# Pooling mixer: the map of the raw stream, with the norm's reciprocals and the shift applied to its output; window masks made in the first FFN; the last inner tile by halves

## The chip, the cores and the metric

One core of one Trainium2 chip. The metric is device time in microseconds for one execution of the program. The engines are named as in the profile: PE is TensorE (matmuls), PEld its weight loads, DVE is VectorE, ACT is ScalarE, POOL is GpSimd, SP is SyncE, which here issues all DMAs.

## The reference, cut to what matters

A two-layer trunk over 1024 latent tokens (a 16 x 64 grid) of 1024 channels. Layer 0 has a recurrent mixer, layer 1 a pooling mixer; each layer then has a gated convolutional FFN with an inner width of 3072. In layer 1:

```python
h = modulate(rms_norm(x, norm_pre_mix), sh_m, sc_m)        # h * (1 + scale) + shift
for g, w in enumerate((2, 4, 8, 16)):                      # 256 channels each
    hg = h[..., g*256:(g+1)*256]
    pooled = window_sum_2d(hg, w) / (cr * cc)              # centred w x w window, clipped
    outs.append((pooled - hg) @ pool_w[g])
y = (concat(outs) + pool_b) * pool_scale
x = x + g_m * rms_norm(y, norm_post_mix)
x = x + g_f * rms_norm(conv_ffn(modulate(rms_norm(x, norm_pre_ffn), sh_f, sc_f)), norm_post_ffn)
```

and the FFN, in both layers:

```python
z = h @ w_up; u, v = z[..., :3072], z[..., 3072:]
u = depthwise_conv3(u) + bias
return (gelu(u) * v) @ w_down
```

## The kernel before, in words

Everything is held with channels on the 128 partitions: the stream X and the work tile Y are `[128, 8, 1024]`, eight channel tiles of 1024 tokens. A half h is 512 tokens (`hs(h)`). Norms are numbered q; q = 3 is the norm behind the first FFN, q = 4 the one ahead of the pooling mixer, q = 5 the one behind it, q = 6 the one ahead of the second FFN, q = 7 the last. `rb_bank` and `ssq_bank` give the PSUM banks of a norm.

**Order of the work.** Each engine has its own list of instructions, written out by hand, and the lists meet only at semaphores. Nothing is planned at run time, so an instruction that waits holds all that stands behind it on its engine. POOL can't read PSUM.

**A norm.** ACT squares the eight tiles (`square`, L1397). The squares are added up on DVE or POOL in one of several forms (`form`): `chain_sums` (L2305), `even_sum` (L2283) and `merge_sums` (L2289) on DVE, `odd_sum` (L1934) and `line_sums` (L1943) on POOL. `column_sums` (L831) on PE then sums over channels: per 512 tokens four fp32 matmuls with one moving column, 8 records in the trace. `norm_root` (L1401, ACT), `norm_scale` (L2320, the reciprocal, DVE) and `spread` (L878, PE), which puts the reciprocal of each token on all partitions of a PSUM bank, follow. Readers of that bank are `scale_tiles` (L2372) and `gate` (L2386) on DVE; `gate_tiles` also adds the even tiles to X (`add_even`, L2396), and POOL adds the odd ones (`add_odd`, L1972).

**FFN.** The loop body (`up`, L1171; `down_pair`, L1191) takes inner tiles in pairs, ten times. Weights and activations are split into high and low fp32r parts, three products each; the low parts of the weights are made on POOL and DVE. The 24th inner tile is alone (`last_up` on ACT and DVE, `down_last` on PE, `last_step` on POOL). Its convolution is a centre tap on ACT (`tap`, L1629), a left tap on DVE (`conv_left`, L2707), both 1024 wide, and a right tap by halves (`last_conv`, L2772). Then gelu (L1638), gate (L2779), high part (L1830) and low part (`last_lo`, L2783). PE's products go by 16 half tiles n (h, m = divmod(n, 8)), of which the first six are computed for the inner tile before and then, once `last_lo` is there, for the last one. DVE adds each to Y (L2631). During this stage `add_rows` (L1962) on POOL finishes the adaLN product of layer 1, out of rows `E_quad` that SP loads and ACT scales (`scale_rows`, L1776), and `later_coefs` on DVE makes its coefficients and the reciprocal window counts `cc` (L2617 to L2622).

**Norm 4.** For half 0 the eight squares are added on PE: `add_squares` (L871) multiplies them by the identity into bank 5, ACT copies the sum (L1870), column sums follow. For half 1 DVE adds six and PE's column sums take the last two.

**Pooling.** `z_tile(i)` (L1272) maps token tile i: out[token, channel] is the sum over k of Y[k, tokens]^T times pool_w, eight fp32 matmuls of 256 columns, into two banks; three pairs of banks are used in turn. Y is the normed, scaled and shifted stream: `scale_tiles(2, 4, h, X, False)` on DVE and `affine(h)` (L1858) on ACT. ACT rounds each result to ZT_hi (`z_hi`, L1864), DVE makes the remainder ZT_lo (`z_lo`, L2948). `window_sums(n)` (L1309, L1291) multiplies the transposed map by 0/1 band masks and count diagonals, 16 times; window 0 writes bank 0. POOL makes the masks (`edge`, L2215 to L2225; `band`, L2230, L2231, L2240) and the diagonals (L2251) behind the first FFN.

## Time and profile before

| | us |
|---|---|
| runs, unprofiled: median of 3 | 2013.16 |
| lowest, highest | 2013.06, 2017.11 |
| profiled execution | 2009.1 |
| its span (first to last recorded instruction) | 2007.4 |
| TensorE busy in it | 1953.0 (97%) |
| mean granted TensorE clock | 0.979 |

Times below are from the span's start. The first FFN's loop ends shortly before 1120, window sums run from 1217, the second FFN starts in the 1270s. A row of the timeline is start, duration, engine, line of the kernel, operation, output and inputs, count, and in brackets how long the engine was idle before it and which engine and instruction ended that. Rows of matmuls count two records per fp32 matmul.

### The profile page before, as it was taken

The page shows a single profiled execution, that of the slowest core. Times are in us where ns is not written, and L with a number is a line of the kernel's source. Part 1 is how long each engine was busy: PE and PEld are TensorE (multiplying, and loading weights), DVE is VectorE, ACT ScalarE, POOL GpSimd, SP SyncE. Part 2 cuts the span into 40 slices and gives each one's busy share as a digit, 9 for nine tenths or more (in the row PEclk, how much of TensorE's full clock was granted, in tenths as well). Part 3 has the DMA queues.
Part 4 walks back from the last instruction along what each step waited for, and adds up shares of the span by engine and source line. Part 5 has one row for each costly group of instructions (what it writes and reads, how often), then busy time and mean ns, then how long its engine had stood idle before and what let it go on. Part 6 is the DMA issues. An engine that isn't in the chain of part 4 may idle for free.

```text
span 2007.4 us, 27912 instructions
## 1 busy us (share of the span) xinstructions
PE 1953.0 (97%) x8766; PEld 1584.6 (79%) x8766; DVE 1669.3 (83%) x1781; ACT 997.8 (50%) x1425; POOL 1267.0 (63%) x846
## 2 busy tenths in 40 slices
PE   8999998999999999999999989899999999999997
PEld 3777776887888888888888768788888888888885
DVE  5588888978799989999998874897888888888888
ACT  5867668456444444444544455573343333343333
POOL 3544244665877778888877762465775655656765
PEclk9999999999999999999999989799999999999998
DMA  8322322540322232322222410211111111111114
GB/s 325 111 87 85 110 84 84 207 161 32 105 74 94 87 101 84 94 84 91 87 94 94 172 49 11 95 53 53 53 52 63 52 52 63 43 61 58 54 55 168
DMA packets 78016, 179.74 MB, mean 90 GB/s; under 512 B 5104, under 2 KB 28944, under 8 KB 77328
## 3 DMA queue, kind: packets, MB, share of 16 engines
q1 hardware_dynamic: 77968, 179.13, 26.1%
q8 instruction: 27, 0.44, 0.1%
q14 instruction: 21, 0.17, 0.0%
HBM read 166.52 MB, written 12.58 MB: 89 GB/s over the span
## 4 chain that ended last, share of the span: by engine, by line
PE 82%; ACT 7%; DVE 5%; issue 3%; POOL 2%; DMA 1%; SPq 1%; ACTq 0%; POOLq 0%; DVEq 0%
PE ps L1171 39%; PE ps L1191 19%; PE ps L772 14%; PE ps L997 2%; PE ps L1272 1%; PE ps L1309 1%; PE ps L831 1%; ACT TH L1524 1%; PE ps L1143 1%; DMA ada_first<-ada 1%; PE ps L878 1%; ACT RA L1527 1%; ACT TH L1534 1%; DVE Y L2386 1%; ACT L1534 1%
## 5 line engine op out<-in xcount | busy, mean ns | idle before, releaser
L2868 DVE TENSOR_TENSOR Y<-Y,ps 128x1024 f32<-128x1024 f32 x280 | 324.2, 1209 | 3.2
L2165 POOL TENSOR_TENSOR So_lo<-So_raw,So_hi 128x512 fp32r<-128x512 f32 x120 | 198.9, 1664 | 198.8 <-DVE So_raw L2804 167.7
L1730 ACT ACTIVATE So_hi<-So_raw 128x512 fp32r<-128x512 f32 x180 | 112.4, 625 | 148.4 <-POOL So_raw L2157 75.9
L1962 POOL TENSOR_TENSOR red<-red,E_quad 128x512 f32<-128x512 f32 x77 | 124.0, 1610 | 65.0 <-ACT E_quad L1776 62.2
L1915 POOL TENSOR_TENSOR WA_lo<-rawA,WA_hi 128x1024 fp32r<-128x1024 f32 x20 | 57.4, 2872 | 163.0 <-DVE u L2508 107.9
L1730 ACT ACTIVATE WB_hi<-rawB 128x512 fp32r<-128x512 f32 x120 | 74.6, 629 | 166.9 <-PE ps L1171 112.8
L1730 ACT ACTIVATE WA_hi<-rawA 128x512 fp32r<-128x512 f32 x120 | 73.1, 625 | 119.6 <-PE ps L1191 83.5
L1171 PE MATMUL ps<-T_hi,So_hi 128*128 128x512 f32 x336 | 131.3, 391 | 0.0
L1171 PE MATMUL ps<-T_hi,So_lo 128*128 128x512 f32 x336 | 130.8, 389 | 0.0
L1171 PE MATMUL ps<-T_lo,So_hi 128*128 128x512 f32 x336 | 130.7, 389 | 0.0
L1171 PE MATMUL ps<-H_hi,WA_hi 128*128 128x512 f32 x336 | 130.7, 389 | 0.0
L1171 PE MATMUL ps<-H_lo,WA_hi 128*128 128x512 f32 x336 | 130.7, 389 | 0.0
L1171 PE MATMUL ps<-H_hi,WA_lo 128*128 128x512 f32 x336 | 130.7, 389 | 0.0
L2165 POOL TENSOR_TENSOR WB_lo<-rawB,WB_hi 128x512 fp32r<-128x512 f32 x80 | 129.8, 1641 | 0.0
L2165 POOL TENSOR_TENSOR WA_lo<-rawA,WA_hi 128x512 fp32r<-128x512 f32 x80 | 104.4, 1305 | 3.8 <-ACT WA_hi L1730 3.8
L772 PE MATMUL ps<-H_hi,WA_hi 128*128 128x512 f32 x252 | 92.2, 412 | 9.0 <-DVE H_lo L2378 6.1
L1634 ACT ACTIVATE S<-S 128x1024 f32<-128x1024 f32 x46 | 48.8, 1062 | 94.6 <-DVE S L2713 94.6
L2856 DVE TENSOR_TENSOR Ub<-t,ps 128x512 f32<-128x512 f32 x84 | 57.8, 688 | 45.1 <-ACT t L1762 35.9
L2707 DVE SCALAR_TENSOR_TENSOR S<-Ub,par,S 128x1024 f32<-128x1024 f32 x48 | 84.4, 1759 | 9.3 <-ACT S L1629 9.3
L2856 DVE TENSOR_TENSOR t<-t,ps 128x512 f32<-128x512 f32 x84 | 57.3, 682 | 40.6 <-PE ps L1171 40.6
L772 PE MATMUL ps<-H_hi,WA_lo 128*128 128x512 f32 x252 | 88.3, 397 | 0.0
L772 PE MATMUL ps<-H_lo,WA_hi 128*128 128x512 f32 x252 | 88.2, 396 | 0.0
(437 smaller groups left out, 6317.8 us busy)
## 6 DMA issues: line engine op xcount, KB each, us to landing
rawA<-wA SPq DMA_DIRECT2D x62, 512.0 KB, 3.2
rawB<-wB SPq DMA_DIRECT2D x62, 512.0 KB, 3.3
E_quad<-ada SPq DMA_DIRECT2D x44, 512.0 KB, 3.4
quad<-ada SPq DMA_DIRECT2D x8, 2048.0 KB, 9.5
rawB<-wC SPq DMA_DIRECT2D x22, 512.0 KB, 3.8
rawA<-wC SPq DMA_DIRECT2D x20, 512.0 KB, 3.7
ada_first<-ada SPq DMA_DIRECT2D x8, 1024.0 KB, 15.1
outT<-X SPq DMA_DIRECT2D x16, 512.0 KB, 3.9
```

The source lines that it names most:

```text
L772: mm = pe.matmul(out, w[:, w_cols:w_cols + P], (hi, lo)[part], start=first and w is W_hi[s] and part == 0, stop=last and w is W_lo[s])
L997: mm = pe.matmul(out, gw[:, gi], src, start=True, stop=True)
L1171: mm = pe.matmul(ps[:, UP_OUT[name]], w[:, at + k * P:at + k * P + P], right[part][:, k], start=k == 0 and w is hi and part == 0, stop=k = ...
L1191: mm = pe.matmul(ps[:, DOWN_OUT[name][m]], w[:, at + m * P:at + m * P + P], TOKEN[name][part], start=name in ("11", "S1", "12") and w is h ...
L1634: A(S[0][:], S[0][:], ACT.Gelu_apprx_tanh).then_inc(gelu_done, 1)
L1730: A(dst[:, at:at + HF], op_source(name), ACT.Copy).then_inc(op_hi, 1)
L1915: TT(W_lo[s][:], raw[s][:], W_hi[s][:].bitcast(F32), ALU.subtract).then_inc(w_ready[s], 1)
L1962: TT(red[:], red[:], E_quad[:, :, k % 2 * P:k % 2 * P + P], ALU.add).then_inc(red_made, 1)
L2165: TT(lo[:, at:at + HF], op_source(name), hi[:, at:at + HF].bitcast(F32), ALU.subtract)\
L2707: STT(S[0][:], Ub[:, 0:T], col("ffn_conv_w", 72 * L + j), S[0][:], ALU.mult, ALU.add)\
L2856: TT(dst, a, b, op).then_inc(up_added, 1)
L2868: TT(at, at, ps[:, bank:bank + 2, :], ALU.add).then_inc(d_added, 1)
```

## The change

Four things.

1. The pooling map runs on X: A = (1 + scale) * norm weight is put into the weights (`pool_s`, made by ACT in `scale_map`), so z = rstd[token] * (X^T pool_s) + shift^T pool_w. `shift_map` on PE multiplies the shift, one column spread over 128 by broadcast, by pool_w into a bank per half, ACT copies it (`copy_shift`) to `z_shift`, and DVE applies reciprocal and shift in place in PSUM (`z_scale`). Tokens are on partitions there, so the reciprocal needs no spreading. `scale_tiles(2, 4, ...)`, `affine` and both `spread(4, ...)` go.
2. Norm 4's squares become lines on POOL with the rest in the column sums (five summed tiles of squares for half 0, three for half 1); `add_squares` goes. Norm 4's first sums stand behind z tile 0, the second behind z tile 3.
3. POOL makes the edges inside `last_step` of layer 0 and the bands between line sums; DVE makes the counts ahead of the last inner tile.
4. The last inner tile's taps go by halves in both layers (`last_tap`, `last_conv_left`, `last_conv`), PE's first products for it wait for u1 and not u3, and DVE's first two additions of its outputs stand before `last_lo(L, 1)`.

```diff
+        SCALED_BASE = {0: 0, 1: 16, 3: 32}
         def form(q, h):
-            if (q, h) == (4, 0):
-                return "acc"
             if q == 0:
                 return "pool"
-            if q == 1 or q and q % 2 == 0:
+            if q == 4:
+                return "line"
...
+        def line_end(q, h):
+            return 4 if (q, h) == (4, 0) else KT - 2
...
+            def shift_map(half):
+                bank = 5 - half
+                if half == 0:
+                    pe.wait_ge(poolw_full, 16)
+                    pe.wait_ge(coef_ready, 4)
+                pe.wait_ge(d_added, half_added("22", 0, PAIRS) + (16 if half else 13))
+                for g in (2 * half, 2 * half + 1):
+                    for k in range(2):
+                        c = (g % 2) * 512 + k * 256
+                        mm = pe.matmul(ps[:, bank, (g % 2) * 256:(g % 2) * 256 + 256],
+                                       M[:, 48 + 2 * g + k:49 + 2 * g + k].to_broadcast([P, P]),
+                                       pool_w[:, half, c:c + 256], start=k == 0, stop=k == 1)
+                mm.then_inc(z_done, 1)
...
 # down_last, PE
-                pe.wait_ge(up_added, added_at("u3", up))
+                pe.wait_ge(up_added, added_at("u1", up))
                 for n in range(6):
-                    if n > 3:
-                        pe.wait_ge(up_added, added_at(("v1", "v0")[n - 4], up))
+                    if n >= 3:
+                        pe.wait_ge(up_added, added_at(("u3", "v1", "v0")[n - 3], up))
...
+                if L == 0:
+                    shift_map(0)
                 square_sums(q, 1)
                 if L == 0:
-                    add_squares(4, 0, (0,))
+                    shift_map(1)
                 spread(q, 1)
...
-            add_squares(4, 0, range(1, KT))
-            norm(4, 0)
+            def z_tile(i):
                 b = 2 * (i % 3)
                 if i == 0:
-                    pe.wait_ge(poolw_full, 16)
+                    pe.wait_ge(zmap_made, KT)
+                if i == 2:
+                    pe.wait_ge(zmap_made, KT + 2)
                 if i >= 3:
                     pe.wait_ge(zt_lo, i - 2)
...
-                                       Y[:, 2 * g + k, i * P:i * P + P], pool_w[:, g // 2, c:c + 256],
+                                       X[:, 2 * g + k, i * P:i * P + P], pool_s[:, g // 2, c:c + 256],
...
-            for i in range(3):
+            z_tile(0)
+            square_sums(4, 0)
+            for i in range(1, 4):
                 z_tile(i)
             square_sums(4, 1)
-            z_tile(3, hook=True)
...
 # ACT
+            def last_tap(L, h):
+                j = FJ - 1
+                act.wait_ge(up_added, added_at("u1" if h else "u0", up_no(L, "A", PAIRS + 1)))
+                act.wait_ge(f_mul, DN * L + FJ - 1)
+                A(S[0][:, hs(h)], Ub[:, 1 + h * HF:1 + h * HF + HF], ACT.Identity, ...)
+            def scale_map(m):
+                act.wait_ge(poolw_full, 16)
+                act.wait_ge(coef_ready, 4)
+                c = m % 4 * 256
+                A(pool_s[:, m // 4, c:c + 256], pool_w[:, m // 4, c:c + 256], ACT.Copy, scale=cA[:, 2, m:m + 1])
...
+                    if L == 0 and 11 <= n < 15:
+                        scale_map(2 * n - 22)
+                        scale_map(2 * n - 21)
...
+            copy_shift(0)
             squares_x(4, 1, 0, (0,))
             norm_root(3, 1)
-            squares_x(4, 1, 0, range(1, KT))
...
+            squares_x(4, 1, 0, range(1, 4))
+            copy_shift(1)
+            squares_x(4, 1, 0, range(4, KT))
+            squares_x(4, 1, 1, range(4))
             norm_root(4, 0)
...
             squares_x(4, 1, 1, range(4, KT))
-            z_hi(1)
-            z_hi(2)
+            for i in range(3):
+                z_hi(i)
             norm_root(4, 1)
-            affine(1)
...
 # POOL
-                    for c in (2, 3):
-                        add_rows(PAIRS + 1, c)
+                    add_rows(PAIRS + 1, 2)
+                    window_edges()
+                    add_rows(PAIRS + 1, 3)
...
                 odd_sums(q, 0)
+                if L == 0:
+                    window_bands(range(3))
                 line_sums(q, 1, (1, 2, 3))
                 add_odd(i, 0, (1,))
                 line_sums(q, 1, (4, 5))
                 add_odd(i, 0, (3, 5, 7))
-                add_odd(i, 1, (1, 3, 5, 7))
+                if L:
+                    add_odd(i, 1, (1, 3, 5, 7))
...
+            line_sums(4, 0, (1, 2))
+            add_odd(1, 1, (1,))
+            line_sums(4, 0, (3,))
+            add_odd(1, 1, (3, 5))
+            line_sums(4, 1, (1,))
+            add_odd(1, 1, (7,))
+            line_sums(4, 1, range(2, line_end(4, 1)))
+            window_bands((3,))
...
+                if n in (2, 3, 4, 5):
+                    pool.wait_ge(z_done, KT + 2)
...
 # DVE
-                    gate_tiles(i, q, 1, range(4))
+                    gate_tiles(i, q, 1, range(KT))
                     norm_scale(4, 0)
...
                 pair_gated(L, "B", PAIRS)
+                if L == 0:
+                    window_counts()
+                last_conv_left(L, 0)
                 for name in ADDED[1:4]:
                     up_add(name, L, "A", p)
-                conv_left(L, FJ - 1)
-                up_add("u3", L, "A", p)
-                up_add("v1", L, "A", p)
                 last_conv(L, 0)
-                up_add("v0", L, "A", p)
+                last_conv_left(L, 1)
+                for name in ADDED[4:]:
+                    up_add(name, L, "A", p)
                 last_gated(L, 0)
+                last_lo(L, 0)
                 last_conv(L, 1)
-                last_lo(L, 0)
+                add_last(L, 0)
                 last_gated(L, 1)
+                add_last(L, 1)
                 last_lo(L, 1)
...
+            def z_scale(i, part=slice(0, D)):
+                dve.wait_ge(z_done, i + 3)
+                if i == 0:
+                    dve.wait_ge(zmap_made, KT + 2)
+                if i % 4 == 0:
+                    dve.wait_ge(rstd_made[i // 4], 5)
+                z = flat((AB01, AB23, AB45)[i % 3])[:, part]
+                STT(z, z, rstd[:, i:i + 1], z_shift[:, part], ALU.mult, ALU.add).then_inc(z_scaled, 1)
...
-            scale_tiles(2, 4, 0, X, False)
-            gate_tiles(1, 3, 1, range(4, KT))
-            chain_sums(4, 1, range(1, chain_end(4, 1)))
...
+            z_scale(0)
+            for i in range(1, 4):
+                z_scale(i)
+                z_lo(i - 1)
             norm_scale(4, 1)
+            z_lo(3)
+            z_scale(4)
+            for i in range(5, KT - 1):
+                z_scale(i)
+                z_lo(i - 1)
+            z_scale(KT - 1, hs(1))
+            z_lo(KT - 2)
+            z_scale(KT - 1, hs(0))
+            for half in (1, 0):
+                z_lo(KT - 1, hs(half))
```

## Rows read from the trace of the kernel before

**Rows 1.** The page's first part: busy time and share of the span by engine.
```profile
PE 1953.0 (97%) x8766; PEld 1584.6 (79%) x8766; DVE 1669.3 (83%) x1781; ACT 997.8 (50%) x1425; POOL 1267.0 (63%) x846
```

**Rows 2.** Windows: stretch, length, busy by engine, PEclk, DMA share, GB/s.
```profile
1179.40:1217.00 37.60, 36.49 (x161) 30.73 (x162) 25.08 (x32) 19.60 (x28) 20.00 (x34) 0.89 0.00 0
...
1164.00:1167.50 3.50, 3.50 (x12) 2.47 (x13) 3.50 (x5) 2.45 (x5) 1.64 (x2) 0.54 0.62 235
...
1177.40:1184.30 6.90, 4.92 (x12) 3.96 (x13) 6.90 (x12) 6.37 (x10) 0.41 (x1) 0.51 0.00 0
...
1194.50:1198.00 3.50, 3.50 (x12) 2.96 (x12) 0.39 (x2) 0.27 (x1) 3.50 (x5) 0.51 0.00 0
```

**Rows 3.** Timeline of PE, layer 0's end to the first window sum.
```profile
1137.65 0.47 PE L772 MATMUL ps<-WB_hi,WA_hi 128*128 128x512 f32 x1 [1.66 <-DVE WB_lo L2783]
...
1150.31 1.05 PE L831 MATMUL ps<-ones,V 128*128 128x1 f32 x8 [0.56 <-DVE V L2295]
...
1153.89 1.16 PE L878 MATMUL ps<-ident,rstd 128*128 128x128 f32 x8 [1.05 <-DVE rstd L2320]
...
1161.20 1.05 PE L831 MATMUL ps<-ones,V 128*128 128x1 f32 x8 [0.70 <-POOL V L1943]
...
1165.87 1.70 PE L878 MATMUL ps<-ident,rstd 128*128 128x128 f32 x8
...
1179.38 13.01 PE L1272 MATMUL ps<-pool_w,Y 128*128 128x256 f32 x48 [2.34 <-ACT Y L1858]
...
1205.57 11.49 PE L1272 MATMUL ps<-pool_w,Y 128*128 128x256 f32 x52 [0.18 <-ACT Y L1858]
1216.71 0.58 PE L1309 MATMUL ps<-band,ZT_hi 128*128 128x512 f32 x1
```

**Rows 4.** Timeline of ACT, 1140 to 1214.
```profile
1140.27 1.34 ACT L1776 ACTIVATE E_quad<-E_quad,silu_c 128x512 f32<-128x512 f32 x2
...
1210.19 1.02 ACT L1864 ACTIVATE ZT_hi<-ps 128x1024 fp32r<-128x1024 f32 x1 [2.43 <-PE ps L1272]
1213.64 1.02 ACT L1864 ACTIVATE ZT_hi<-ps 128x1024 fp32r<-128x1024 f32 x1 [2.43 <-PE ps L1272]
```

**Rows 5.** Timeline of DVE, 1128 to 1168.
```profile
1128.52 2.17 DVE L2707 SCALAR_TENSOR_TENSOR S<-Ub,par,S 128x1024 f32<-128x1024 f32 x1 [1.31 <-ACT S L1629]
...
1151.68 1.25 DVE L2619 TENSOR_SCALAR cc<-cc 128x32 f32<-128x32 f32 x1
...
1167.60 1.41 DVE L2386 SCALAR_TENSOR_TENSOR Y<-Y,cG,ps 128x512 f32<-128x512 f32 x2
```

**Rows 6.** Timeline of SP, and DMA issues 1100 to 1230 (size, time to landing).
```profile
1146.89 0.37 SPq L747 DMA_DIRECT2D pool_w<-poolw  x1
...
pool_w<-poolw SPq DMA_DIRECT2D x1, 1024.0 KB, 6.8
```

**Rows 7.** Timeline of POOL, and one group of 1140 to 1230 (busy, mean ns).
```profile
1141.07 2.73 POOL L1962 TENSOR_TENSOR red<-red,E_quad 128x512 f32<-128x512 f32 x2 [4.72 <-ACT E_quad L1776]
...
1165.47 1.58 POOL L1972 TENSOR_TENSOR X<-X,Y 128x512 f32<-128x512 f32 x1 [1.42 <-DVE Y L2386]
...
1187.95 0.53 POOL L2215 MEMSET edge<- 128x512 f32 x1
...
1192.98 0.30 POOL L2225 MEMSET edge<- 64x256 f32 x1
...
L1943 POOL TENSOR_TENSOR V<-V,S 128x512 f32<-128x512 f32 x4 | 5.2, 1290 | 1.9 <-ACT S L1397 1.6
```

**Rows 8.** Groups of DVE over the span: busy us, mean ns of one.
```profile
L2948 DVE TENSOR_TENSOR ZT_lo<-ps,ZT_hi 128x1024 fp32r<-128x1024 f32 x8 | 9.7, 1223 | 8.7 <-ACT ZT_hi L1864 8.6
...
L2386 DVE SCALAR_TENSOR_TENSOR ps<-Y,cG,ps 128x512 f32<-128x512 f32 x8 | 6.0, 756 | 1.1 <-PE ps L878 0.5
```

**Rows 9.** Timelines of DVE and PE, last inner tile of layer 1.
```profile
1961.40 2.99 DVE L2707 SCALAR_TENSOR_TENSOR S<-Ub,par,S 128x1024 f32<-128x1024 f32 x1 [1.32 <-ACT S L1629]
...
1965.13 0.47 PE L772 MATMUL ps<-F_hi,WC_hi 128*128 128x512 f32 x1 [0.34 <-DVE t L2856]
```

More of the change, by code:

```diff
@@ L104, in build_trunk @@
         sq0 = sb("sq0", [P, T])
-        W_lo = {"A": sb("WA_lo", [P, D], F32R), "B": sb("WB_lo", [P, D], F32R), "C": WC_lo}
+        W_lo = {"C": WC_lo}
+        W_lo["A"], = overlay(("WA_lo", [P, D], F32R))
+        z_shift = sb("z_shift", [P, D])
+        W_lo["B"] = sb("WB_lo", [P, D], F32R)
         S = [sb("S0", [P, T]), S1]
@@ L435, in form, with spreads_to @@
         def form(q, h):
-            if (q, h) == (4, 0):
-                return "acc"
             if q == 0:
                 return "pool"
-            if q == 1 or q and q % 2 == 0:
+            if q == 4:
+                return "line"
+            if q == 1 or q % 2 == 0:
                 return "chain"
             return "line" if q in (3, 7) and h else "tree"
+        def line_end(q, h):
+            return 4 if (q, h) == (4, 0) else KT - 2
+        def spreads_to(q):
+            return q - (q > 4)
         def adds_to(q, h, chain, pairs, tree=0):
-            each = {"chain": chain, "tree": pairs + tree, "line": KT - 3, "acc": 0, "pool": KT - 1}
-            return sum(each[form(n, h)] for n in range(q))
+            each = {"chain": chain, "tree": pairs + tree, "pool": KT - 1}
+            return sum(line_end(n, h) - 1 if form(n, h) == "line" else each[form(n, h)] for n in range(q))
         def chain_end(q, h):
@@ L458, in evens_to @@
         def evens_to(q, h):
-            each = {"tree": 3, "line": 0, "acc": 0, "pool": 0}
+            each = {"tree": 3, "line": 0, "pool": 0}
             return sum(chain_end(n, h) - 1 if form(n, h) == "chain" else each[form(n, h)] for n in range(q))
@@ L853, in square_sums @@
                     column_sums(q, h, *total, True, False)
-                    for p in (KT - 2, KT - 1):
+                    for p in range(line_end(q, h), KT):
                         pe.wait_ge(sq_made[h], 8 * q + p + 1)
@@ L1284, in window_sums @@
                     pe.wait_ge(band_ready, 3 * len(WINDOWS))
+                if n == 2:
+                    pe.wait_ge(zt_lo, KT + 1)
                 if n >= 4:
@@ L1385, in square @@
                         act.wait_ge(ssq_done[1], q)
-                    if (q, h) == (4, 0) and p > 3:
-                        act.wait_ge(acc_done, p - 3)
                 elif q == 0:
@@ L1767, in pair_tap @@
                 tap(L, 2 * p + 1 + "AB".index(s))
+            def scale_map(m):
+                act.wait_ge(poolw_full, 16)
+                act.wait_ge(coef_ready, 4)
+                c = m % 4 * 256
+                A(pool_s[:, m // 4, c:c + 256], pool_w[:, m // 4, c:c + 256], ACT.Copy, scale=cA[:, 2, m:m + 1])\
+                    .then_inc(zmap_made, 1)
             def scale_rows(q, c):
@@ L1818, in last_up @@
                 round_f(L, FJ - 2)
+                last_tap(L, 0)
                 round_down(L, FJ - 2)
```

145 lines of the change are left out of this document (67 added, 78 removed).

## The prediction

> **What bounds the kernel now.** The page's first part [rows 1]: TensorE is busy 97% of the span, so time comes off only where it idles, runs slowly, or does work that can go. The two FFN loops are full and hardly touched, so I read the stretches by stage [rows 2]. From 1160.5 to 1217.0, between the last down product of layer 0 and the first window sum, TensorE is poorly used: idle time in the first 18.9 us, and from the first z tile on a granted clock of 0.89. In the low stretches it is near 0.5, that is 1.2 GHz and not 2.4.
>
> TensorE's timeline [rows 3] gives the order. Products end at 1160.5 (0.70 idle before 1161.20). Then come norm 3's column sums, the adding of norm 4's squares by identity matmuls, norm 4's root, reciprocal and spreading, DVE's scaling, ACT's shift, and only then, at 1179.38, the first z tile. A z tile is 8 fp32 matmuls, 16 records, and costs 3.455 us at the full clock (ACT's ZT_hi, 1210.19 to 1213.64 [rows 4]). Eight are 27.6, but they last until 1217.06, since the second half waits for its own norm. Window sums start at 1216.71, and everything from there to the second FFN hangs on that start.
>
> **z stage.** The map now multiplies X itself. Removed are 16 scalings on DVE, 16 shifts on ACT, the identity matmuls and two spreads. How early can tile 0 start?
>
> - Before the products end, DVE loses the three count operations between its adds 9 and 10 (one took 1.25 at 1151.68 [rows 5]; about 1.6 with the other two and gaps). So norm 3's reciprocal is earlier, and the spread, which waited 1.05 [rows 3], waits no more: products end near 1159.3.
> - shift_map(0) is four fp32 matmuls 256 wide, half a z tile: 1.73, to 1161.0. It waits for pool_w, with the sums queued behind it; pool_w was issued at 1146.89 and landed after 6.8 [rows 6], 5 us ahead of need, and its place among SP's loads stays. Copying the result (128x512, 0.6) on ACT, with squares behind it, and the eight scale_map pieces (128x256 each) lie in idle gaps of the ACT.
> - Column sums of norm 3, right half: 24 records, which took 1161.20 to 1164.15. Again 2.95: 1164.0. The 1.2 us won before is spent.
> - shift_map(1): 1.73 at the full clock, 3.46 at half. Sums one column wide have let the clock fall: 0.54 granted from 1164.0, right after them [rows 2]. I take 3.4: 1167.4. Then the spread, 1.4 (1.70 when it lay partly in the low stretch [rows 3]): 1168.8. DVE began the gates that read it at 1167.60 [rows 5], so they lose 1.2.
>
> From here TensorE in order:
>
> - Tile 0: 3.46, to 1172.3. X of half 0 is complete; POOL's last addition to it ran from 1165.47 for 1.58 [rows 7].
> - Wait for POOL. Behind that addition stand two line sums, one X addition and a third line sum, each between 1.29 and 1.60 (the lower is the mean of a line sum [rows 7]): 1172.2 to 1173.5. DVE's own X additions contend, so I take 1173.3: a wait of 1.0.
> - Sums of norm 4, left half: one total and four squares, 40 records, 4.9 at full, 9.8 at half clock. The clock went down about 3 us after the earlier stretch of sums began [rows 2, 3]. Two fifths at full: 7.1, to 1180.4. The reciprocal follows at 1181; DVE has done the 12 gate and addition operations ahead of it by about 1178.
> - Tiles 1 to 3: 10.37, and 3 us at half clock at their start lose 1.6 (as from 1194.5 to 1198.0, at 0.51 [rows 2]): 1192.4.
> - Sums of norm 4, right half: 24 records, 2.95: 1195.3. POOL's five line sums for it are done by 1187.
> - Tiles 4 to 7: 13.82, and 1.5 lost in the same way: 1210.6.
> - The tail is new. Window sum 0 writes the banks of tile 6, and z_lo(6) stands on DVE behind the scaling of half of tile 7: 0.75 and 1.22 [rows 8], together 2.0: 1212.6. Before, the window sums followed with no gap.
>
> So the windows start at 1212.6 instead of 1216.7: **4.1 us earlier**.
>
> z_scale works in place in PSUM, 128x1024, a form that the trace lacks. It lies between 0.756, which a 512 wide one takes [rows 8], and twice that, 1.51; I take 1.3, nearer to twice. With z_lo's 1.22 DVE then needs 2.5 per tile against TensorE's 3.46. ACT needs 1.02. Tile and chain, 3.46 + 1.3 + 1.02 + 1.22 = 7.0, fit in the 10.4 that three buffers give. At either bound TensorE doesn't wait: nothing, beyond the tail.
>
> The masks' edges, ten operations from 1187.95 to 1193.28 [rows 7], were hidden under z tiles. They go to the 4.72 in which POOL waited for ACT ahead of E_quad's last addition [rows 7], and the bands to its waits for squares. No gain, and the last addition is 0.6 late; the matmuls that read its result come later. The diagonals in spare wait for the last z tile, with layer 1's first remainders behind them; those are needed only in the second FFN.
>
> **Last inner tile by halves, both layers.** In layer 0 TensorE waits 1.66 at 1137.65 for WB_lo [rows 3]. The chain behind it is tap, left tap (2.17 at 1128.52 [rows 5]), u3, v1, right tap. By halves a tap is 0.75 alone, so up to 1.7 could go. But POOL has WC_lo, WA_lo and two additions back to back there, and DVE operations with both operands in SBUF end just after one of POOL's: the left tap took 2.17 where twice 0.756 would do, and 2.99 in layer 1 [rows 9]. There are more such operations now, with the three counts ahead of u2. Walked through on that footing: counts to 1125.1, left tap 1128.1, u1 1130.0, right tap 1131.1, second left tap 1134.1, v0 1136.1, WB_lo 1138.8, which is 1.2 later than TensorE's start at 1137.65. Unblocked it is ready by 1135.8, 1.7 earlier. Either is met again: ACT's first square waits for E_quad until 1140.27 [rows 4], and the total of squares that TensorE wanted at 1150.31, idle 0.56 [rows 3], comes when it came. Price in layer 0: nothing, with bounds of 0.5 gained and 1 lost.
>
> The Trainium skill (SBUF — State Buffer, "SBUF: two separate sides") says that the port pair which DVE and GpSimd share is an exclusive lock: the second comer stands still for the first one's whole instruction. By that rule the walk to 1138.8 is the one that happens, and by free sharing the one to 1135.8. The trace leans to the lock, with 2.17 and 2.99 for the same operation.
>
> In layer 1 TensorE waited only 0.34, for u3 behind the 2.99 tap [rows 9]. It now needs u1 first, which was there before that tap began at 1961.40, and u3 only for its fourth product: **0.4 earlier**, and from there to the end TensorE and then DVE follow.
>
> **Sum.** 4.1 + 0.4 = 4.5. The profiled execution took 2009.1 (span 2007.4 and 1.7 around it), which gives 2004.6. The runs' median is 4.06 above it, so 2013.16 - 4.5 = **2008.7**. A measurement here can tell about 0.2%, 4.0 us, from no change; the forecast stands just beyond.
>
> **Rivals.**
>
> - *The clock holds better.* shift_map(1) takes 1.7 less, the spread 0.4 less, the left sums 2.2 less, tiles lose 1.5 less, and layer 0's halves give 0.5: up to 6 more than forecast. For it: the left sums have a full tile ahead of them. Against: after each stretch of sums in this stage the clock fell. Gain 6.5 to 11, middle 8.5: 2004.7.
> - *Absorbed.* All 40 records run at half clock (2.7 more), and the tiles after them stay at it for 7 us, as from 1177.4 to 1184.3 [rows 2] (1.9 more). That leaves 0 to 3, some 2012. For it: POOL is slowed by each of DVE's additions, and an idle TensorE brings the clock down sooner. If the change does not do what it says, because DVE's queue and not the norm held the first tile back, the time is here too.
> - *Slower, by the shared port.* In both layers DVE stands behind whole POOL operations in the last inner tile. Five of its operations (three taps, gate, remainder) by up to 2.4 make 12 per layer at most. It decides from 5.5 in sum, the gain of 4.5 and the 1 that layer 0 hides. At 4 per layer: 8 - 5.5 = 2.5 slower, 2015.7; up to 2018 with the counts in front. Against it: the u additions between them read PSUM and are not held.
>
> **Numbers.** Forecast case (gain 3 to 6.5, so 2006.6 to 2010.2) 0.45; better clock 0.22; absorbed 0.20; slower 0.13. The range over them is 2003.0 to 2014.0. Two thirds of the first case, 0.31, lie beyond 4.0: faster 0.22 + 0.31 = 0.53; same 0.14 + 0.20 = 0.34; slower 0.13.
>
> **What would show it.** Right: products end near 1159.3 and the first z tile starts near 1168.8; 40 records of sums take 5 to 9 us, in part at half clock; a gap of 2 before the first window sum, near 1212.6; WB_lo no earlier in layer 0; the loops the same. Wrong: sums at the full clock throughout; TensorE waiting over 2 us for POOL; a z tile waiting for z_lo; WB_lo over 3 late; products ending after 1160.5.

## The result, and the profile after

The changed kernel took 2018.04 us (median of 20 runs, 2013.49 to 2026.37), the kernel before 2012.17 on the same chip (20 runs). The ratio is 1.003, 95% interval 1.002 to 1.0039: **slower** by 0.3%, which is small but clear of the noise, where a gain of 0.2% was forecast. A second comparison (after_again, below) gave 1.004, 1.0028 to 1.0052. The profiled execution took 2018.32, its span is 2016.6; that of before was 2007.4, an execution 4 us under its median, so the 9.2 us between the two traces overstate the loss.

The page's first part [answers rows 1]:

```profile
PE 1956.5 (97%) x8782; PEld 1593.6 (79%) x8782; DVE 1677.2 (83%) x1772; ACT 991.4 (49%) x1421; POOL 1289.3 (64%) x854
```

TensorE's share says nothing. The windows by stage do: first before, then after (stretch, length, busy by engine, PEclk, DMA share, GB/s). The four stages are the products behind the second pass of the last tile, from there to the first z tile, the z tiles, and the window sums.

```profile
1137.60:1160.50 22.90, 21.23 (x102) 17.09 (x102) 19.98 (x37) 12.38 (x20) 12.60 (x10) 1.00 0.84 321
1160.50:1179.40 18.90, 14.60 (x66) 9.62 (x65) 13.52 (x21) 9.07 (x18) 8.31 (x6) 0.86 0.23 84
1179.40:1216.70 37.30, 36.19 (x160) 30.45 (x161) 25.08 (x32) 19.60 (x28) 20.00 (x34) 0.89 0.00 0
1216.70:1262.00 45.30, 43.16 (x287) 40.55 (x285) 24.77 (x37) 27.13 (x39) 16.41 (x11) 0.92 0.04 13
```

```profile
1139.50:1167.00 27.50, 23.98 (x103) 19.47 (x104) 21.09 (x35) 15.32 (x28) 19.68 (x23) 0.88 0.68 258
1167.00:1173.90 6.90, 6.90 (x50) 6.49 (x48) 5.92 (x10) 5.06 (x12) 4.16 (x4) 1.00 0.63 229
1173.90:1220.70 46.80, 41.58 (x195) 36.94 (x193) 29.67 (x31) 14.63 (x22) 26.14 (x28) 0.85 0.00 1
1220.70:1268.80 48.10, 45.96 (x284) 43.00 (x284) 25.40 (x39) 26.64 (x39) 16.34 (x11) 0.86 0.04 12
```

The products take 4.6 us longer, the way to the first z tile 12.0 less, the z tiles 9.5 more and the window sums 2.8 more, at 0.86 of the clock against 0.92. From the end of the products to the windows the trace of before has 56.2 us and this one 53.7: of the map's gain 2.5 are there. Ahead of it and behind it more than that goes.

TensorE's timeline [answers rows 3]:

```profile
1139.50 0.47 PE L783 MATMUL ps<-WB_hi,WA_hi 128*128 128x512 f32 x1 [1.81 <-DVE WB_lo L2847]
...
1154.23 1.05 PE L842 MATMUL ps<-ones,V 128*128 128x1 f32 x8 [2.63 <-DVE V L2347]
...
1166.88 1.89 PE L885 MATMUL ps<-pool_w,M 128*128 128x256 f32 x8
1168.60 0.95 PE L842 MATMUL ps<-ones,V 128*128 128x1 f32 x8
1169.41 1.93 PE L842 MATMUL ps<-ones,S 128*128 128x1 f32 x16
1171.20 1.97 PE L885 MATMUL ps<-pool_w,M 128*128 128x256 f32 x8
1173.01 1.05 PE L894 MATMUL ps<-ident,rstd 128*128 128x128 f32 x8
1173.90 3.62 PE L1288 MATMUL ps<-pool_s,X 128*128 128x256 f32 x16
1180.76 8.69 PE L842 MATMUL ps<-ones,sq 128*128 128x1 f32 x40 [3.25 <-POOL sq L1975]
1189.31 12.92 PE L1288 MATMUL ps<-pool_s,X 128*128 128x256 f32 x48
...
1204.66 14.06 PE L1288 MATMUL ps<-pool_s,X 128*128 128x256 f32 x64
1220.70 0.50 PE L1327 MATMUL ps<-band,ZT_hi 128*128 128x512 f32 x1 [1.97 <-DVE ZT_lo L3026]
```

TensorE's idle time has grown in three places: 2.63 for the total of norm 3's squares (0.56 before), 3.25 for GpSimd's line sum in the z stage, 1.97 ahead of the windows. Behind each of them stands a stretch at 1.2 GHz in which it is busy:

```profile
1157.20:1163.20 6.00, 5.36 (x17) 4.59 (x18) 3.25 (x7) 2.06 (x4) 3.83 (x3) 0.50 0.09 35
1177.50:1181.00 3.50, 0.25 (x3) 0.24 (x2) 3.50 (x5) 1.18 (x2) 3.50 (x4) 0.91 0.00 0
1181.00:1194.00 13.00, 13.00 (x51) 12.10 (x52) 5.86 (x6) 3.88 (x7) 11.50 (x10) 0.50 0.00 1
1221.70:1224.50 2.80, 2.80 (x8) 2.25 (x7) 0.89 (x2) 2.13 (x3) 1.54 (x1) 0.50 0.00 0
```

The long one, 13 us, holds all 40 sum records and the start of tile 1. Added up over the whole span in windows of 2 us, TensorE is busy at half clock for 59.5 us in the trace of before and for 74.5 in that of after: 15 more, and 7.5 of the 9.2 us are half of that. That the clock is lower holds beyond single traces: the granted clock, averaged over all executions, is 0.9785 for the kernel before and 0.9750 for the changed one.

Where the low stretches lie does not hold beyond single traces. The trace of after_again is a second one of the same changed kernel:

```profile
1169.99 3.48 PE L885 MATMUL ps<-pool_w,M 128*128 128x256 f32 x8
...
1179.06 7.98 PE L842 MATMUL ps<-ones,sq 128*128 128x1 f32 x40 [1.25 <-POOL sq L1975]
...
1217.56 0.50 PE L1327 MATMUL ps<-band,ZT_hi 128*128 128x512 f32 x1 [1.98 <-DVE ZT_lo L3026]
```

Here shift_map(1) runs at 1.2 GHz (3.48 in place of 1.97) and the wait for GpSimd is 1.25 in place of 3.25. The products behind the second pass take 25.3 us (27.5 in the first trace, 22.9 before), the way from their end to the windows 51.9, and the window sums 46.8, with no half clock behind the same gap of 2.0. The wait for the total is 2.65, as in the first trace. So a difference of one or two microseconds between stages of single traces can be chance, and the ratios decide.

Why the total is late shows in the queues of ScalarE and VectorE in the last tile [they answer rows 4 and 5]:

```profile
1141.87 0.63 ACT L1863 ACTIVATE WB_hi<-S 128x512 fp32r<-128x512 f32 x1 [1.16 <-DVE S L2843]
1142.52 1.28 ACT L1866 ACT_TABLE_LOAD   x1
1143.82 1.34 ACT L1808 ACTIVATE E_quad<-E_quad,silu_c 128x512 f32<-128x512 f32 x2
1145.06 0.61 ACT L1414 ACTIVATE V<-Y 128x512 f32<-128x512 f32 x1
```

```profile
1128.97 2.90 DVE L2836 SCALAR_TENSOR_TENSOR S<-Ub,par,S 128x512 f32<-128x512 f32 x1
1131.79 2.88 DVE L2830 SCALAR_TENSOR_TENSOR S<-Ub,par,S 128x512 f32<-128x512 f32 x1
...
1138.56 0.80 DVE L2847 TENSOR_TENSOR WB_lo<-S,WB_hi 128x512 fp32r<-128x512 f32 x1 [0.76 <-ACT WB_hi L1863]
1139.28 0.77 DVE L2836 SCALAR_TENSOR_TENSOR S<-Ub,par,S 128x512 f32<-128x512 f32 x1
1140.47 0.69 DVE L2684 TENSOR_TENSOR Y<-Y,ps 128x512 f32<-128x512 f32 x1 [0.42 <-PE ps L783]
1141.08 0.76 DVE L2843 TENSOR_TENSOR S<-S,V 128x512 f32<-128x512 f32 x1
```

ScalarE runs from its second WB_hi through the table load and E_quad to the first square without a pause: the square comes 3.19 behind the start of WB_hi. And WB_hi waits for the gate of the second half. On VectorE the right tap that this gate needs now stands behind WB_lo of the first half, which itself waits for ScalarE (before, the tap came first), and between tap and gate stands an addition that waited 0.42 for TensorE. In the kernel before, the same queue (E_quad's row is in [rows 4]):

```profile
1138.98 1.28 ACT L1833 ACT_TABLE_LOAD   x1
...
1141.52 0.62 ACT L1397 ACTIVATE V<-Y 128x512 f32<-128x512 f32 x1
```

There the table load began 1.33 after the second pass, now 3.02 after it.

### The profile page after: what moved, and what is told of

It reads as the page before. It is cut to its first block and busy times, and to the rows that moved or that the text cites. A ratio compares the mean times of both kernels' runs of the same rounds, so it can differ in the third digit from the quotient of the medians.

```text
span 2016.6 us, 27965 instructions
## 1 busy us (share of the span) xinstructions
PE 1956.5 (97%) x8782; PEld 1593.6 (79%) x8782; DVE 1677.2 (83%) x1772; ACT 991.4 (49%) x1421; POOL 1289.3 (64%) x854
## 5 line engine op out<-in xcount | busy, mean ns | idle before, releaser
L2223 POOL TENSOR_TENSOR So_lo<-So_raw,So_hi 128x512 fp32r<-128x512 f32 x120 | 208.0, 1740 | 200.1 <-DVE So_raw L2868 169.0
L783 PE MATMUL ps<-H_hi,WB_hi 128*128 128x512 f32 x220 | 79.3, 402 | 5.8 <-ACT Y L1554 3.9
```

What stands on the lines that cost most here:

```text
L783: mm = pe.matmul(out, w[:, w_cols:w_cols + P], (hi, lo)[part], start=first and w is W_hi[s] and part == 0, stop=last and w is W_lo[s])
L2223: TT(lo[:, at:at + HF], op_source(name), hi[:, at:at + HF].bitcast(F32), ALU.subtract)\
```

## The experiments

All ratios are against the kernel before on the same chip, with 95% intervals; "clock" is the granted clock averaged over all executions of a kernel.

**e1_whole: the halves undone.** VectorE's end of queue is that of the kernel before again, with one centre tap and one left tap, and TensorE's first products wait for u3 again; map, masks and counts stay. VectorE's part:

```
-last_conv_left(L, 0)
 for name in ADDED[1:4]:
     up_add(name, L, "A", p)
+conv_left(L, FJ - 1)
+up_add("u3", L, "A", p)
+up_add("v1", L, "A", p)
 last_conv(L, 0)
-last_conv_left(L, 1)
-for name in ADDED[4:]:
-    up_add(name, L, "A", p)
+up_add("v0", L, "A", p)
 last_gated(L, 0)
+last_conv(L, 1)
 last_lo(L, 0)
-last_conv(L, 1)
-add_last(L, 0)
 last_gated(L, 1)
-add_last(L, 1)
 last_lo(L, 1)
```

> The changed kernel with one part undone: the last inner tile is convolved whole again (one centre tap, one left tap), and VectorE's queue ends as in the kernel before. Map, masks, counts stay. Theory A (the last tile's new order on VectorE lets ScalarE's second WB_hi, its table load and so the squares of norms 3 and 7 come late, and the products wait for the total of the squares and then run at half clock): products of the last tile, from WB's pass to their end, fall from 27.5 to about 23 us in layer 0 and from 21.4 to about 20 in layer 1; the time comes to about 1.000 of the kernel before, 2012. Theory B (the window counts on VectorE, or the lock between VectorE and GpSimd, delay it): the stage stays near 27 us and the time at 1.003, 2018. Theory C (the window edges on GpSimd delay its sums): as B.

Ratio 1.0011 (1.0 to 1.0023), clock 0.9757: some 0.2% of the loss goes. Layer 1's products are back at 19.9 us from 21.4. Layer 0's are 26.5, not 23: the wait for the total fell from 2.63 only to 1.56, and a stretch at half clock still followed. So the halves in this order cost, and something else in the same stage does too.

**e2_before_halves: the kernel before with the halves alone** (the same edit the other way round).

> The kernel before with this one part added: the last inner tile's taps by halves and the new order on VectorE in both layers. Theory A: the products after the second pass of the last tile take 4 to 5 us longer in layer 0 and about 1.5 in layer 1, and the time is 1.002 to 1.003 of the kernel before. Theories B and C: nothing of it is in this kernel, so the ratio is 1.000.

Ratio 0.9998 (0.9986 to 1.0009), clock 0.9785. Theory A's time is refuted here, and its mechanism is not: the trace shows the wait for the total at 2.54 and products of 26.8 us. But the second pass began 1.8 us earlier relative to the tile's first product (4.1 against 5.9 us), and the way to the first z tile was 2.1 shorter (16.8 against 18.9), since VectorE and ScalarE set that stage and not TensorE. So in this kernel the loss is covered by other queues. That it lies bare once the map has taken their work away is read from the two traces.

**e3_order: the halves kept, VectorE's order as before.**

```
 last_gated(L, 0)
-last_lo(L, 0)
 last_conv(L, 1)
-add_last(L, 0)
+last_lo(L, 0)
 last_gated(L, 1)
-add_last(L, 1)
 last_lo(L, 1)
+add_last(L, 0)
+add_last(L, 1)
```

> The changed kernel with the taps still by halves, but the end of VectorE's queue in the order of the kernel before: gated 0, last_conv(1), WB_lo(0), gated 1, WB_lo(1), and both additions behind them. Theory A, in its narrow form (it is the order, not the split taps): second WB_hi on ScalarE about 1.2 us earlier, the wait of the products for the total at most 1 us, the stage 23 to 24.5 us, time 1.000 to 1.001. If the split taps themselves are what costs, the stage stays at 26 or more and the time at 1.002 to 1.003.

Ratio 1.0008 (0.9996 to 1.0019), clock 0.9765. Products 23.45 in layer 0 and 19.72 in layer 1, wait for the total 1.11 and no half clock in the stage: the narrow form of theory A holds. It was the order and not the split. The way from the products' end to the windows was 55.6 us in this trace, which is of an execution 3 us above its kernel's median.

**e6_sums: norm 4's left sums behind the second z tile.**

```
 z_tile(0)
+z_tile(1)
 square_sums(4, 0)
-for i in range(1, 4):
+for i in range(2, 4):
     z_tile(i)
```

> The changed kernel with TensorE's sums of norm 4, first half, behind the second z tile in place of the first. Theory D (TensorE waits 3.3 us there for GpSimd's last line sum while there is work for it): the wait goes, the z stage from its first product to the windows is 2 to 3 us shorter, the time 1.001 to 1.002 of the kernel before. Rival: VectorE's scaling of the first tile needs the same norm and becomes the wait, so that the stage is less than 1 us shorter and the time stays at 1.003.

Ratio 1.0015 (1.0002 to 1.0029), clock 0.9759. The wait for GpSimd is gone, the z tiles take 40.2 us from the first to the windows in place of 46.8 (43.4 in the changed kernel's second trace), and no z tile waits for VectorE. The rival (VectorE becomes the wait) falls.

**e10_map: the map alone**, with the tile whole, the counts behind the coefficients, and edges and bands behind the line sums on GpSimd.

```
 line_sums(4, 1, range(2, line_end(4, 1)))
-window_bands((3,))
+window_edges()
+window_bands(range(4))
```

> The kernel before with the mixer's map and its sums alone: last tile whole, window counts behind the coefficients, window masks behind the line sums on GpSimd, as in the kernel before or behind its new work. Theory F (what is lost is TensorE's clock: its mean over all executions fell from 0.9785 in the kernel before to 0.975 in the changed one, the same as before with the halves alone, so the fall comes with the map's stage, where TensorE now stands 3.3 us for GpSimd's line sum and runs the 40 columns behind it at half clock): the stage from the end of the products to the windows is 2 to 3 us shorter than before's 56.2, the mean clock 0.976, the time 1.000 to 1.001. Rival (my prediction's sum for the map was right, and the masks, counts and halves ahead of it lose it): 0.998 of the kernel before, clock 0.978 or more.

Ratio 0.9998 (0.9988 to 1.0008), clock 0.9772. Products 22.9, as before; the wait for GpSimd is 3.25 and the gap ahead of the windows 1.97 here as well. The map as written gains nothing, and it holds neither the whole loss nor the forecast gain. Theory F's time came true and its stage did not: from the products' end to the windows the trace has 57.1 us and not 2 to 3 less than 56.2. That trace is of an execution 6 us above the kernel's median, and its last four z tiles hold 6.5 us at half clock.

**e5_masks: only edges and bands moved back** in the changed kernel, as above.

> The changed kernel with the window masks behind the line sums on GpSimd in place of inside the first feed-forward part. Theory C (4.8 us of edges ahead of the odd sums and 4.3 us of bands behind them make GpSimd late for X's additions and its line sums of norm 4): TensorE's wait for GpSimd in the z stage falls from 3.3 us to 1 or less, time 1.001 to 1.002. Theory F with the masks hidden: wait and ratio as in the changed kernel, 1.003, or more if the masks now end after the z tiles.

Ratio 1.0017 (1.0008 to 1.0026), clock 0.9758. By the ratios the masks cost 0.13 to 0.23%, with overlapping intervals against the changed kernel's first ratio and none against its second. Theory C's time holds. Its wait for GpSimd was 1.07, but that does not bear it out: shift_map(1) ran at half clock here (3.34), and the changed kernel itself has 1.25 where it does so. The wait for the total was still 2.19. Their mark is on VectorE, ahead of the reciprocal that the spread waits for; VectorE and then GpSimd in the changed kernel:

```profile
1154.88 0.75 DVE L2407 SCALAR_TENSOR_TENSOR cA<-M,par 128x8 f32<-128x8 f32 x2
1155.56 1.26 DVE L2413 TENSOR_TENSOR dM<-M 128x4 f32<-128x4 f32 x1
```

```profile
1154.40 1.13 POOL L2190 TENSOR_TENSOR band<-edge 128x448 fp32r<-128x448 f32 x1
1155.52 1.28 POOL L1975 TENSOR_TENSOR V<-V,acc 128x512 f32<-128x512 f32 x1
```

cA starts beside a band and ends with it; dM, of 4 columns, runs exactly as long as GpSimd's addition, which the bands have made to follow without a pause. Here, with the bands gone, dM takes 0.15.

**e4_counts: only the three counts moved back.**

```
-if L == 0:
-    window_counts()
 last_conv_left(L, 0)
```

> The changed kernel with the window counts on VectorE behind the coefficients again. They are three small instructions of 0.2 us; theory B (they hold up the left tap, and what hangs on it) allows 0.6 us twice at most: time 1.0025 to 1.003. All other theories: 1.003, as the changed kernel.

Ratio 1.0027 (1.0015 to 1.0039), clock 0.9754: no effect that could be told. The counts are not 0.2 us each where the change puts them: in the changed kernel they take 1.27, 1.23 and 0.19. The second pass did begin 2.5 us earlier (4.1 against 6.6 us behind the tile's first product), and the products, still waiting for the total, took 26.2.

**e9_best: three mends in the changed kernel.** The order of e3, the sums of e6, and in VectorE's queue:

```
-z_scale(KT - 1, hs(1))
 z_lo(KT - 2)
+z_scale(KT - 1, hs(1))
 z_scale(KT - 1, hs(0))
```

> The changed kernel with three mends: end of VectorE's queue in the order of the kernel before (as e3_order), sums of norm 4 behind the second z tile (as e6_sums), and on VectorE the remainder of tile 6 ahead of the scaling of tile 7. Theory F: products of the last tile in 23.5 us, end of products to windows in 48 to 49 us (before 56.2), so 6 to 7 us less than the kernel before in these stages; if the clock stays at 0.976 to 0.977 half of that is given back and the ratio is 0.998 to 0.999. Rival (any saving there is given back in full by the clock of the windows and of the second feed-forward part): 1.000 or more, with a mean clock of 0.975.

Ratio 0.996 (0.9945 to 0.9974), clock 0.9788: more than the better of the two forecasts. Products to windows 47.15 (56.2 before), window sums 45.2. The clock is back at that of before (0.9784 on this chip).

**e12_no_tail: without the third mend.**

> Of the three mends only two: VectorE's order and the sums behind the second z tile; the remainder of tile 6 stays behind the scaling of tile 7. The gap ahead of the windows was 2.0 us in both e6_sums and the changed kernel. If the mend of the tail is worth its shorter gap (about 0.5 us) the ratio is 0.996; if it is what let the clock stay up in the windows, 0.998 or more.

Ratio 0.998 (0.9969 to 0.9992), clock 0.9779. TensorE's first window sum, in e12_no_tail and then in e9_best:

```profile
1218.28 0.50 PE L1327 MATMUL ps<-band,ZT_hi 128*128 128x512 f32 x1 [1.97 <-DVE ZT_lo L3027]
```

```profile
1215.27 0.50 PE L1327 MATMUL ps<-band,ZT_hi 128*128 128x512 f32 x1 [0.25 <-DVE ZT_lo L3027]
```

The gap goes from 1.97 to 0.25. Exchanging two operations was worth 4 us by the ratios, though their intervals leave anything from nothing to 9; 1.7 are the gap. The window sums (46.7 against 45.2 us) differ by 1.5 more, but not right behind the gap: there both run at full clock, and the longer low stretch is some 23 us later (1241.5 to 1252 against 1240 to 1247). Over all traces the window sums take 46.6 to 48.2 us behind a gap of 2 (ten traces, mean 47.4) and 45.2 to 46.9 without it (seven, mean 46.1); five of the ten have 3 to 3.5 us at half clock right behind the gap, five have none. So the gap seems to cost about a microsecond beyond its length, on average and not each time.

**e13_best_whole: e9_best with the tile whole.**

> The mended kernel (e9_best) with the last tile convolved whole, VectorE's queue as in the kernel before; masks and counts stay early. With the masks early and the tile whole the products took 26.5 us in e1_whole, against 23.5 with the halves in e3_order. If that difference belongs to the halves (they bring the additions no earlier, but the squares of the second half less late), the stage is again 25 us or more and the ratio 0.997 to 0.998. If it was the chance of one clock fall, 23.5 to 24 us and 0.996, as e9_best.

Ratio 0.997 (0.996 to 0.998), products 26.5 again. Here the halves are worth 0.1% in the right order. With the masks behind the sums and the counts behind the coefficients it is the other way: e16_best_counts, with halves, has 0.9963, and e15_map_mended, without them and otherwise the same, 0.9955. The intervals overlap in both pairs, so no worth of the halves is shown.

**e11_best_masks: e9_best with the masks moved back.**

> The mended kernel (e9_best) with the window masks behind the line sums again. Theory C (the masks on GpSimd hold VectorE's small operations and the sums: even sum 0.87 in place of 0.69 us, dM 1.27 in place of 0.15): products 23 us or less, wait for the total under 0.5 us, time 0.995 of the kernel before. Rival: behind the line sums the masks end after the z tiles or slow VectorE's work there, and the ratio is 0.997 or more.

Ratio **0.9945** (0.9932 to 0.9959), 2000.28 us median of 6, clock 0.9802: the fastest kernel of all, 11 us under the kernel before. Its windows by stage, as above:

```profile
1137.60:1159.00 21.40, 20.97 (x103) 17.50 (x104) 18.40 (x34) 14.63 (x27) 12.74 (x10) 1.00 0.88 335
1159.00:1167.60 8.60, 8.60 (x50) 7.69 (x49) 7.07 (x10) 5.27 (x12) 6.44 (x5) 0.80 0.52 184
1167.60:1206.10 38.50, 38.25 (x195) 34.15 (x193) 27.35 (x29) 13.79 (x21) 29.88 (x42) 0.91 0.00 1
1206.10:1251.20 45.10, 42.96 (x284) 40.42 (x284) 26.06 (x40) 27.24 (x40) 17.27 (x14) 0.92 0.04 13
```

TensorE is idle for 0.25 us in the z tiles' 38.5, and the products end 1.5 earlier behind the second pass than before.

**after_again: the changed kernel once more.**

> The changed kernel once more, on the chip of these runs, so that the mended kernels are held against it: 1.003 of the kernel before and a mean clock of 0.975 by every theory. A ratio under 1.0015 would mean that the first comparison overstated the loss.

Ratio 1.004 (1.0028 to 1.0052), clock 0.9746. The loss is real.

**e14_map_sums and e15_map_mended: the map alone, with the sums of e6, then with the tail too.**

> The map alone (e10_map) with the sums of norm 4 behind the second z tile. If the wait for GpSimd's line sum (3.25 us and the half clock behind it) is what took the map's gain, the ratio goes from 0.9998 to 0.998 or less. If not, it stays within 0.001 of 0.9998.

> As e14_map_sums, with the remainder of tile 6 ahead of the scaling of tile 7 as well. If the map's own two gaps are the cause, the ratio is 0.9955 to 0.997 (the gap ahead of the windows goes from 1.97 to 0.25 us), about that of e11_best_masks without its halves. If the halves and masks were needed for the gain, 0.998 or more.

Ratios 0.998 (0.9965 to 0.9995) and **0.9955** (0.9939 to 0.9972), clocks 0.9776 and 0.9789. So the two gaps were the map's own, and with them mended it gives 0.45% (0.28 to 0.61), more than the 0.2% forecast, with no help from halves or masks. The last step, the tail alone, is worth 0.25% here and was worth 0.2% in e9_best. TensorE in e15_map_mended:

```profile
1172.43 7.07 PE L1288 MATMUL ps<-pool_s,X 128*128 128x256 f32 x32
1179.34 5.58 PE L842 MATMUL ps<-ones,sq 128*128 128x1 f32 x40
...
1210.95 0.50 PE L1327 MATMUL ps<-band,ZT_hi 128*128 128x512 f32 x1 [0.25 <-DVE ZT_lo L3019]
```

The 40 sum records take 5.58 here and 8.69 or 7.98 in the changed kernel.

**e16_best_counts: e11_best_masks with the counts moved back.**

> The kernel of e11_best_masks (0.9945) with the window counts behind the coefficients again, as in the kernel before. If the three counts ahead of the left tap were a cost of their own (they make WB_lo late: 6.4 us from the first product of the last tile to the second pass, 4.1 in e4_counts without them), the pass comes 2 us earlier, the products take no more than 1 us longer, and the ratio is 0.9935 to 0.994. If the products wait for the total of squares by as much as the pass starts earlier, 0.9945 as e11_best_masks, and the counts cost nothing.

Ratio 0.9963 (0.9952 to 0.9975): if anything slower than with the counts early. The spread waits again, for the reciprocal that stands behind the counts:

```profile
1155.27 1.16 PE L894 MATMUL ps<-ident,rstd 128*128 128x128 f32 x8 [1.02 <-DVE rstd L2371]
```

In e11_best_masks the spread has no such wait. The counts' early place looks right, though the intervals still overlap (e11_best_masks 0.9932 to 0.9959, this 0.9952 to 0.9975); neither forecast, a gain or the same ratio, came true.

**The total's wait** separates order and masks. It is TensorE's idle time before the column sums of norm 3, left half, layer 0:

| last tile | masks behind the sums | masks early |
|---|---|---|
| whole | 0.55 (e10), 0.56 (before) | 1.56 (e1) |
| halves, the change's order | 2.19 (e5), 2.54 (e2) | 2.63 (after) |
| halves, the order of before | 0.38 (e11) | 1.11 (e3) |

The other runs lie beside these: 0.54 and 0.59 (e15, e14) beside 0.55, 1.67 (e13) beside 1.56, 2.62 and 2.65 (e6, after_again) beside 2.63, 1.11 and 1.15 (e9, e12) beside 1.11. In before, e2, e10, e14 and e15 the counts stand behind the coefficients. Where only their place differs, moving them back lengthens the wait: 2.85 (e4) against 2.63, 0.93 (e16) against 0.38.

## Why the prediction was wrong

The forecast was 2008.7, faster; it is slower by 0.3 to 0.4%, some 6 us.

**Earlier spread, products end 1.2 sooner.** Right only where masks and order are mended too: in e11_best_masks the spread waits no more and the products take 21.4 us in place of 22.9. With the bands early it still waits 1.05 (e3, e9) although the counts are gone from its path, since cA and dM, ahead of the reciprocal, have become as much longer. In the changed kernel the late total adds to that.

**The last tile by halves, "price in layer 0: nothing". This is the step that failed at the highest price.** The text let a late or early WB_lo be met again, because "ACT's first square waits for E_quad until 1140.27". The row cited shows no idle time before E_quad: it began at 1140.27 because the table load ahead of it had just ended, not because a transfer was due. A time of the queue was taken for a fixed one. The part moved WB_hi of the second half, hence the table load, and the square with it: 5.6 us behind the second pass instead of 3.9 (1145.06 less 1139.50; 1141.52 less 1137.65). The bounds, 0.5 gained and 1 lost, were too narrow: the products took 4.7 longer (2.4 in the second trace), 2.1 of it wait for the total and much of the rest a half clock from 1157.2 to 1163.2. The order costs 0.2 to 0.3%, 4 to 6 us, by e3_order (1.0008) against the two comparisons of the changed kernel (1.003 and 1.004). What the new order puts ahead of the second right tap (a remainder that waits for ScalarE) and ahead of the second gate (an addition that waits for TensorE) was not costed; only the taps were.

**Layer 1, 0.4 earlier.** The start of the second pass is earlier by 0.16 (4.24 to 4.08), but the products take 1.5 longer there for the same reason, with a wait for the total of 1.47 in place of 0.50:

```profile
1979.25 0.63 ACT L1863 ACTIVATE WB_hi<-S 128x512 fp32r<-128x512 f32 x1 [1.69 <-DVE S L2843]
1979.90 1.28 ACT L1866 ACT_TABLE_LOAD   x1
```

With the old order (e3, e9, e11) both stretches together are 0.37 shorter than before: the 0.4 was right for the split, and was lost by the order.

**Masks, hidden at no cost.** Probably wrong: they cost 0.13 to 0.23% by e5 against the changed kernel and 0.15% by e11 against e9, where the intervals overlap. The prediction had E_quad's last addition 0.6 late and looked only at who reads its result. It is 0.7 late (4.1 in place of 3.4 behind the second pass, e1 against e10), and what matters stands beside and behind it: VectorE's first even sum, next to GpSimd's odd one, took 1.82 in e1 and 1.17 in e10, and two sums next to bands 0.88 and 0.83 for 0.69. That is 1.0, the whole difference of the total's wait, 1.56 against 0.55. The Trainium skill (SBUF — State Buffer, "SBUF: two separate sides") says that the two engines' shared port pair is an exclusive lock; the trace agrees, with dM's 1.26 beside GpSimd's 1.28. The prediction had weighed this for the taps and not for the masks. Its walk through the taps holds in sum: left tap 1.79, right tap 2.90, second left tap 2.88, where it had 3.0, 1.1 and 3.0. The second pass started 6.57 behind the tile's first product in place of 5.89, 0.7 later where 1.2 was walked.

**The z stage, 4.1 earlier.** Of it 1.2 were the products' end. The rest was summed nearly right: 53.3 us from the products' end to the windows forecast (1159.3 to 1212.6), 53.7 in the trace and 51.9 in the second, and the tail gap of 2.0 was 1.97. GpSimd's last line sum, for which TensorE waits, was forecast 14.0 behind the products' end and came after 13.7. Inside, errors cancelled in part. shift_map(1) ran at the full clock, 1.97 for 3.4, and TensorE was through with tile 0 about 2.5 sooner than walked, so the wait for GpSimd was 3.25 for 1.0. In the second trace shift_map(1) took 3.48, and the wait was 1.25, nearly as forecast. GpSimd began the four operations in question 0.6 sooner behind the products than walked and took 6.5 for 6.2, since two of its line sums took 1.82 each beside VectorE's operations:

```profile
1174.17 3.64 POOL L1975 TENSOR_TENSOR sq<-sq 128x512 f32<-128x512 f32 x2
1177.77 1.26 POOL L2004 TENSOR_TENSOR X<-X,Y 128x512 f32<-128x512 f32 x1
1178.99 1.72 POOL L1975 TENSOR_TENSOR sq<-sq 128x512 f32<-128x512 f32 x1
```

What the sum had too small in both traces is the 40 records: 8.69 and 7.98 for 7.1. (By its own words the sum should be 6.8, with 3 us at full clock, or 7.8, with two fifths of the records at full; 7.1 is neither.) The half clock around them lasts 13 to 14 us in the five traces with the wait of 3.25, 10 us in the two with 1.07 and 1.25, and 6.5 to 7 where they stand behind the second tile and wait for nothing. z_scale took 1.29 for the 1.3 assumed.

Even so the map alone did not gain its share: e10_map has 0.9998 where the forecast's 4.1 would give 0.998. So this was a second step that failed. The sum took the wait and the gap as the idle time they show and stopped at the first window sum; closing both was worth 0.43% by the ratios (e10 to e15), some 8.7 us for 1.25 to 3.25 and 1.7 us of idle time.

**The windows, costed at nothing.** They took 2.85 longer on the same work, at 0.86 of the clock for 0.92, and 1.5 longer in the second trace. That the gap of 2.0 could be followed by a stretch at half clock was a term missing altogether. e9 against e12 and e15 against e14 put the tail at 4 and 5 us for a gap 1.7 shorter, but the intervals do not exclude 1.7.

**The rivals.** "Slower, by the shared port" gave 2015.7 to 2018, and the time lies at its upper end, but its mechanism was a wait of TensorE for WB_lo, "over 3 late". That wait hardly grew (1.66 to 1.81), and in e4_counts, where the second pass starts 2.5 us earlier, nothing is won. So it was right in sign for another cause, though what the masks cost does seem to come from the shared port. The range stated, 2003.0 to 2014.0, left this rival out although it had a chance of 0.13. "Absorbed" had the records at half clock right (wholly so in the first trace) and fits the map alone (0.9998).

What stays open: the ratios of the single parts are uncertain by about 0.1% each. That the order and the two gaps cost is shown; the shares of order, masks and gaps aren't exact, and the masks' own is at the edge of the noise. How much of each gap's price is the idle time and how much the clock is read from traces, not shown by an experiment. And why the clock fell in one execution and not in another of the same kernel, behind the same instructions and the same gap, no run shows.

## What to carry to other kernels

A row without idle time in front of it is no fixed point: ask what stands ahead of it on its own queue, and whether the change moves that. After a sum of idle times, go on past its end: behind a gap a busy TensorE can run at 1.2 GHz for some microseconds, so a gap can cost more than its length. It did so in the traces here on average, not each time. Two cheap exchanges (sums behind a tile that is ready, a remainder ahead of a scaling) took the map alone from no gain to 0.45%; with order and masks mended as well, the changed kernel's loss of 0.3% became a gain of 0.55%. Take a second trace of the same kernel before explaining a stage by a clock that one trace shows. When a change has several parts, hold each against the kernel with the others in place as well: the halves in their new order cost nothing in the kernel before and 0.2% beside the map.

## What the runs showed of the hardware

- The granted clock, averaged over executions, goes with small differences in time but is not all of them: 0.9746 and 0.9750 went with ratios of 1.004 and 1.003, 0.9802 with 0.9945, but 0.9785 with both 1.0 (before) and, within 0.0004, 0.9955 to 0.9963 (e9, e15, e16), whose stages are shorter. Among the executions of the kernel before alone, 0.982 and 2006.4 us stand at one end and 0.974 and 2017.7 at the other.
- Column sums one column wide can hold the full clock: 24 records took 2.7 us at 1168.60 with the granted clock at 1.00, and the half clock that the forecast had put behind them did not come there. In e11_best_masks, e15_map_mended and after_again it did (0.80 over the stage), with the same instructions, and the last of these is the same kernel.
- The same gap of 1.97 to 1.98 us ahead of the same window sums was followed by 3 to 3.5 us at half clock in five traces (after, e1, e5, e10, e14) and by none in five (after_again, e3, e4, e6, e12).
- VectorE's scaling in place in PSUM, 128x1024 with a per-partition factor, takes 1.29, and 0.76 at 512.
